# Expert matmuls of an encoder layer in pairs of weight units: the order of TensorE, ScalarE and VectorE, four raw slots and six pairs of split tiles

## What is computed

```python
xg = xt[ids]
return (jax.nn.silu(xg @ wg) * (xg @ wu)) @ wd
```

## Time and profile before

| | |
|---|---|
| time, median of 3 runs | 2544.8 us (2542.86 to 2548.42) |
| profiled execution: its own time | 2542.72 us |
| profiled execution: span | 2540.9 us |
| busy: PE | 2404.7 us, 95% |
| busy: DVE | 1933.9 us, 76% |
| busy: ACT | 1697.1 us, 67% |
| one expert, first matmul to first matmul (1329.75 to 1429.42) | 99.67 us |

### The profile page before, as it was taken

How to read it: one execution, slowest core, us unless ns; L and a number is a source line. 1 busy time by engine, 2 the same in 40 slices (tenths; PEclk the granted TensorE clock), 3 DMA queues, 4 the chain that set the end, 5 groups by cost and what they waited for, 6 DMA issues and landing times.

```text
span 2540.9 us, 51701 instructions
## 1 busy us (share of the span) xinstructions
PE 2404.7 (95%) x21830; PEld 2199.9 (87%) x21830; DVE 1933.9 (76%) x2311; ACT 1697.1 (67%) x2379; POOL 257.5 (10%) x175
## 2 busy tenths in 40 slices
PE   7999997998979949999999999999999999999997
PEld 5776884785757739999999999999999999999997
DVE  4621035884873379899999998998999999989986
ACT  6311224573443248888888888888888888888885
POOL 3312111110122000000000000000000000000000
PEclk9999996997889969999999999999999999999999
DMA  4122201002023369999999999999999999999993
GB/s 125 34 73 95 67 17 35 1 3 66 1 91 123 112 244 336 359 372 343 367 364 350 367 360 349 382 343 357 374 345 365 366 348 367 360 349 382 345 365 126
DMA packets 325114, 624.33 MB, mean 246 GB/s; under 512 B 11828, under 2 KB 48788, under 8 KB 324884
## 3 DMA queue, kind: packets, MB, share of 16 engines
q1 hardware_dynamic: 317220, 602.78, 66.6%
q0 software_dynamic: 7664, 18.25, 3.6%
HBM read 597.23 MB, written 23.69 MB: 244 GB/s over the span
## 4 chain that ended last, share of the span: by engine, by line
PE 60%; issue 3%; DVE 1%; DMA 0%; POOL 0%; POOLq 0%; ACT 0%
PE ps L1754 26%; PE ps L1782 13%; PE ps L1760 13%; PE ps L1788 6%; PE ps L1799 1%; PE ps L1736 1%; DVE wlo L1920 0%; DVE vals L1928 0%; DVE index L1931 0%; DMA out_rows<-yr,idxT 0%; DVE aff L1930 0%; POOL out_rows L1705 0%; POOL xg L1695 0%; POOLq L1674 0%; PE ps L1720 0%
## 5 line engine op out<-in xcount | busy, mean ns | idle before, releaser
L1920 DVE TENSOR_TENSOR wlo<-raw,whi 128x2048 bf16<-128x2048 f32 (+1 forms) x436 | 963.8, 2223 | 57.7 <-ACT whi L1826 54.9
L1826 ACT ACTIVATE whi<-raw 128x2048 fp32r<-128x2048 f32 (+1 forms) x436 | 804.9, 1859 | 37.6 <-PE ps L1788 37.6
L1754 PE MATMUL ps<-xx,whi 128*128 128x264 f32 x4512 | 616.2, 289 | 4.6 <-DVE xx L1971 4.6
L1754 PEld LDWEIGHTS ps<-xx,whi 128*128 128x128 f32 x4512 | 564.2, 189 | 4.8 <-DVE xx L1971 4.8
L1760 PE MATMUL ps<-xb,wlo 128*128 128x132 bf16 x4512 | 312.9, 221 | 0.0
L1782 PE MATMUL ps<-hx,whi 128*128 128x264 f32 x2256 | 312.4, 290 | 0.0
L1782 PEld LDWEIGHTS ps<-hx,whi 128*128 128x128 f32 x2256 | 283.9, 189 | 0.0
L1760 PEld LDWEIGHTS ps<-xb,wlo 128*128 128x128 bf16 x4512 | 263.2, 97 | 13.7
L1920 DVE TENSOR_TENSOR wlo_last<-raw,whi_last 128x2048 bf16<-128x2048 f32 (+1 forms) x108 | 240.6, 2228 | 13.1 <-ACT whi_last L1826 13.1
L1836 ACT ACTIVATE low<-ps 128x264 f32<-128x264 f32 x352 | 137.7, 391 | 135.8 <-PE ps L1760 122.1
L1826 ACT ACTIVATE whi_last<-raw 128x2048 fp32r<-128x2048 f32 (+1 forms) x108 | 201.5, 1866 | 9.3 <-PE ps L1788 9.3
(11 more groups left out here) (237 smaller groups left out, 3438.6 us busy)
## 6 DMA issues: line engine op xcount, KB each, us to landing
raw<-in_w_gate SPq DMA_DIRECT2D x80, 2048.0 KB, 12.6
raw<-in_w_up SPq DMA_DIRECT2D x80, 2048.0 KB, 10.3
raw<-in_w_down SPq DMA_DIRECT2D x64, 2048.0 KB, 10.9
raw<-in_w_down SPq DMA_DIRECT2D x32, 1536.0 KB, 8.2
raw<-in_w_gate SPq DMA_DIRECT2D x16, 1024.0 KB, 9.0
raw<-in_w_up SPq DMA_DIRECT2D x16, 1024.0 KB, 11.7
w<-in_w_in SPq DMA_DIRECT2D x28, 512.0 KB, 5.2
zv_rows<-qn SPq DMA_DIRECT2D x24, 256.0 KB, 2.0
```

The costliest lines, as they stand in the source:

```text
L1754: pe.matmul(banks(b + i)[:, 0:2 * C2], w[:, k, i * P:(i + 1) * P], xx[:, k], start=(k == 0), stop=False, skip_group_check=True)
L1826: nc.scalar.activation(shaped(whi[n % R_SPLIT], u), unit_raw(raw, ex, u), ACT.Copy).then_inc(hi_ready, 1)
L1920: nc.vector.tensor_tensor(shaped(wlo[n % R_SPLIT], u), unit_raw(raw, ex, u), shaped(whi[n % R_SPLIT], u).bitcast(F32), ALU.subtract).then_ ...
```

## The change

TensorE takes the units two at a time: high pass of both, then low pass of both. ScalarE and VectorE go by steps of a pair: at step p both copies or sums of pair p-1 come first, then `split_hid` of pair p-2, one split, `silu` or `gate`, and the remaining splits of the step (two in most steps, one where the table steps down at p = 4 and 8, three at p = 13 and 15). The raw ring has four slots in place of five, and the memory goes to a sixth pair of `whi` and `wlo`. `add_low` of an odd unit has one more wait, on the `gate` of the pair before (`us` must have been read), which stands ahead of it on the same engine. `split_rows` moves to the end of step 13.

```diff
-NR = 5
-R_SPLIT = 5
+NR = 4
+R_SPLIT = 6
...
-    wlo = [tiles(f"wlo{i}", [P, 2 * KD * P], BF16) for i in range(R_SPLIT - 1)]
+    wlo = [tiles(f"wlo{i}", [P, 2 * KD * P], BF16) for i in range(R_SPLIT - 2)]
...
+    wlo.append(after("wlo_next", [P, 2 * KD * P], BF16))
...
-    SPLIT_X = TURN_X + 2
+    SPLIT_X = UNITS_UP // 2 + 2
-    OUT_STEPS = {2: 0, 3: 1, 4: 2, 5: 3}
+    OUT_STEPS = {3: 0, 5: 1, 7: 2, 9: 3}
-    def lead(u):
-        return 4 if u < 6 or u >= 30 else 3 if u < 13 or u >= 27 else 2
-    def made(ex, u):
-        return min(UNITS * N_EXP, UNITS * ex + u + lead(u) + 1)
+    def made(ex, p):
+        return min(UNITS * N_EXP, UNITS * ex + 2 * p + (6 if p < 4 or p >= 15 else 5 if p < 8 or p >= 13 else 4))
```

On TensorE (`up` and `down` are each cut into a high and a low function):

```diff
-                for u in range(UNITS):
-                    if u < UNITS_UP:
-                        up(ex, u)
-                    else:
-                        down(ex, u)
+                for u in range(0, UNITS, 2):
+                    high, low = (up_high, up_low) if u < UNITS_UP else (down_high, down_low)
+                    high(ex, u)
+                    high(ex, u + 1)
+                    low(ex, u)
+                    low(ex, u + 1)
```

On ScalarE (VectorE has the same skeleton, with `add_low`, `split_low` and `gate`):

```diff
-                for u in range(UNITS):
-                    if 1 <= u <= UNITS_UP:
-                        copy_low(ex, u - 1)
+                for p in range(UNITS // 2):
+                    if 1 <= p <= PAIRS:
+                        copy_low(ex, 2 * p - 2)
+                        copy_low(ex, 2 * p - 1)
...
-                    while ahead < made(ex, u):
+                    if 2 <= p < PAIRS + 2:
+                        split_hid(ex, p - 2)
+                    if ahead < made(ex, p):
                         split_high(ahead)
                         ahead += 1
-                    if 1 <= u <= UNITS_UP and u % 2 == 1:
-                        silu(ex, u // 2)
-                    if u >= 4 and u % 2 == 0 and (u - 4) // 2 < PAIRS:
-                        split_hid(ex, (u - 4) // 2)
-                    if u == SPLIT_X and ex + 1 < N_EXP:
+                    if 1 <= p <= PAIRS:
+                        silu(ex, p - 1)
+                    while ahead < made(ex, p):
+                        split_high(ahead)
+                        ahead += 1
+                    if p == SPLIT_X and ex + 1 < N_EXP:
                         split_rows(ex + 1)
```

In VectorE's `add_low`:

```diff
+                if kind == 1 and PAIRS * ex + u // 2 >= 1:
+                    dve.wait_ge(hid_ready, PAIRS * ex + u // 2)
```

More of the change, by code:

```diff
@@ L1737, in turn_rows, with up_high @@
                 mm.then_inc(xT_done, 1)
-            def up(ex, u):
+            def up_high(ex, u):
                 t, kind = divmod(u, 2)
@@ L1755, in up, with up_low @@
                                   skip_group_check=True)
+            def up_low(ex, u):
+                n = UNITS * ex + u
                 pe.wait_ge(lo_ready, n + 1)
+                b = bank_set(ex) + 2 * (u % 2)
                 w = shaped(wlo[n % R_SPLIT], u)
@@ L1762, in up, with down_high @@
                 mm.then_inc(unit_done, 1)
-            def down(ex, u):
+            def down_high(ex, u):
                 dg, d = divmod(u - UNITS_UP, len(DOWN_PARTS))
@@ L1783, in down, with down_low @@
                                   skip_group_check=True)
+            def down_low(ex, u):
+                dg, d = divmod(u - UNITS_UP, len(DOWN_PARTS))
+                c0, cn = DOWN_PARTS[d]
+                n = UNITS * ex + u
+                b = (other_set(ex), bank_set(ex))[dg]
                 pe.wait_ge(lo_ready, n + 1)
@@ L1803, in _ @@
             for ex in range(N_EXP):
-                for u in range(UNITS):
-                    if u < UNITS_UP:
-                        up(ex, u)
-                    else:
-                        down(ex, u)
-                    if u in OUT_STEPS and ex >= 1:
-                        turn_outputs(ex - 1, OUT_STEPS[u])
-                    if u == TURN_X and ex + 1 < N_EXP:
+                for u in range(0, UNITS, 2):
[4 more added lines that the diff above has]
+                    low(ex, u + 1)
+                    if u + 1 in OUT_STEPS and ex >= 1:
+                        turn_outputs(ex - 1, OUT_STEPS[u + 1])
+                    if u + 1 == TURN_X and ex + 1 < N_EXP:
                         turn_rows(ex + 1)
@@ L1889, in _ @@
             for ex in range(N_EXP):
-                for u in range(UNITS):
-                    if 1 <= u <= UNITS_UP:
-                        copy_low(ex, u - 1)
-                    if u == DG0_END:
+                for p in range(UNITS // 2):
+                    if 1 <= p <= PAIRS:
+                        copy_low(ex, 2 * p - 2)
+                        copy_low(ex, 2 * p - 1)
+                    if 2 * p == DG0_END:
                         copy_ylow(ex, 0)
-                    if u == 0 and ex >= 1:
+                    if p == 0 and ex >= 1:
                         copy_ylow(ex - 1, 1)
-                    while ahead < made(ex, u):
+                    if 2 <= p < PAIRS + 2:
+                        split_hid(ex, p - 2)
+                    if ahead < made(ex, p):
                         split_high(ahead)
                         ahead += 1
-                    if 1 <= u <= UNITS_UP and u % 2 == 1:
-                        silu(ex, u // 2)
-                    if u >= 4 and u % 2 == 0 and (u - 4) // 2 < PAIRS:
-                        split_hid(ex, (u - 4) // 2)
-                    if u == SPLIT_X and ex + 1 < N_EXP:
+                    if 1 <= p <= PAIRS:
[4 more added lines that the diff above has]
+                    if p == SPLIT_X and ex + 1 < N_EXP:
                         split_rows(ex + 1)
-                    if u - 1 in OUT_STEPS and ex >= 1:
-                        gated_rows(ex - 1, OUT_STEPS[u - 1])
+                    if 2 * p - 1 in OUT_STEPS and ex >= 1:
+                        gated_rows(ex - 1, OUT_STEPS[2 * p - 1])
             copy_ylow(N_EXP - 1, 1)
@@ L1988, in _ @@
             for ex in range(N_EXP):
[L1989 to L1994, removed]
+                for p in range(UNITS // 2):
+                    if 1 <= p <= PAIRS:
+                        add_low(ex, 2 * p - 2)
+                        add_low(ex, 2 * p - 1)
+                    if 2 * p == DG0_END:
                         add_ylow(ex, 0)
-                    if u == 0 and ex >= 1:
+                    if p == 0 and ex >= 1:
                         add_ylow(ex - 1, 1)
-                    if u >= 5 and u % 2 == 1 and (u - 5) // 2 < PAIRS:
-                        split_hid(ex, (u - 5) // 2)
-                    while ahead < made(ex, u):
+                    if 2 <= p < PAIRS + 2:
+                        split_hid(ex, p - 2)
+                    if ahead < made(ex, p):
                         split_low(ahead)
                         ahead += 1
-                    if u == SPLIT_X and ex + 1 < N_EXP:
+                    if 1 <= p <= PAIRS:
+                        gate(ex, p - 1)
+                    while ahead < made(ex, p):
+                        split_low(ahead)
+                        ahead += 1
+                    if p == SPLIT_X and ex + 1 < N_EXP:
                         split_rows(ex + 1)
```

## The result

The changed kernel takes 2765.41 us (median of 4, 2763.85 to 2767.72) against 2544.09 us: ratio 1.0867, 95% interval 1.0849 to 1.0886. It is slower by 221 us. The forecast of 2725 us had the sign and most of the size; 40 us are missing from it.

A forecast was written before the change was run, and what follows sets the result against it. It took TensorE, busy throughout each expert, as today's bound; after the change, a chain through ScalarE's and VectorE's lists. 16 x 9.5 (up) + 15 x 2.0 (down) = 182 us on 2542.7 gave 2725 us, range 2655 to 2790.

The forecast's parts named there:

- What bounds the kernel: Expert stage, some 1,590 us: TensorE busy throughout (66.27 us up part, 33.40 down part), waiting for nothing.
- the chain: Up part, ScalarE's and VectorE's ordered lists: 14.09 us between releases, 7.05 a pair against 5.88; +9.5 us an expert.
- The pairs on TensorE: Up part: the even unit's sum comes 6.0 us after pair start, over 5.80; as a rival alone 2595 us, chance 0.06.
- The switches: TensorE, float32 to bf16 runs halved: 0.08 us saved a pair; as a rival alone 22 us gained, 2521, chance 0.04.
- The tokens: Down part: TensorE waits 2.4 us for the next expert's split tokens; down part +2.0 us, for 15 experts.
- Four slots: Raw-weight ring: taken as 0, upper end 48 us; as a rival, late loads give 2735 to 2775, chance 0.14.
- The clock: Rival: TensorE's idling drops it to 1.2 GHz, up part 128 us, total above 3400, chance 0.04; otherwise clock 1.00.
- signs of being right: Expected in the profile: PE idle some 1.2 us a pair, 2 us wait on xx, expert of 111 us, clock 1.00.
- The range: Whole kernel: own range 2658 to 2773, widened to 2655 to 2790 us.
- link error: Up part: 0.1 us more or less on each link pair, 16 x 10 x 0.1 = 16 us in all.
- the head of an expert: Start of each expert: late units there, for which the upper end was raised from 2773 to 2790 us.

## Why the prediction was right, and where it was not

- **What bounds the kernel, and the chain.** Right in place and nearly in size: 14.14 us for two pairs against 14.09, the releaser `gs`, whi ahead of DVE's first split with 1.37 us of idle time. The run with one split moved ahead shows that the chain is the cause: it takes whi out of it, two pairs fall to 12.68 us, and 165 us go. Over a whole expert's up part the links are 0.5 us longer than their sum (10.0 against 9.5).
- **The pairs on TensorE.** The forecast derived the wait from them: a sum that comes 0.2 us too late even with both engines free, and then the chain. The run with units one by one shows that they are not needed for it: the chain alone, with a whole unit between sum and reuse, costs as much. The Trainium skill asks that independent groups of matmuls rotate through the banks, so that the evacuation of one overlaps the matmuls of the next ("Perfetto Trace Analysis", section "Matmuls"); in that run they rotate as before, and the wait is there all the same, 1.87 us at the pair shown.
- **The switches.** 0.08 us a pair was taken; a pair without waits is 5.81 (5.80 forecast), and the down part alone in pairs shows 0.07.
- **The tokens.** 2.4 forecast, 2.38 measured, and shown to be `xx` by the run that takes it away. Taken away alone, it gave 6 us, as a late load took its place; with the loads shortened as well, 63.
- **Four slots.** 0 was right for the changed kernel, but the windows of 10.5 us that the forecast called slack at the end of the down part are where the loads become late (18 us at most from issue to landing) as soon as PE comes 4 us earlier.
- **The clock.** This is the term that was mis-sized. The forecast weighed it as a rival, all up parts at 1.2 GHz and above 3400 us, and put it at 0 otherwise, with a clock of 1.00 among its signs of being right. It fell in part: 34 us in all, 1.5 us a fall, once or twice an expert.
- **The range.** That 2765 lies inside 2655 to 2790 is in part luck. The forecast's own link error was 16 us; the room above that was put there for the slots and the head of an expert, which took nothing, and the clock and the longer links filled it.

## What to carry to other kernels

When two engines feed a third in order, follow the chain through their lists, from the result that is waited for back to the instruction that stands in front of it, around the loop and for every consumer: here a copy, one split and two splits of lead cost 1.2 us a pair though every engine had idle time, and one instruction moved, with a little less lead, gave back three quarters, a part of it by the clock. In this kernel grouping like passes was worth its switches (0.07 us a pair) only where no bank had to come free between the groups; there it paid a little, 0.3%, with one more split tile. Before a wait is taken out, see what stands right behind it: the tokens' wait hid late loads.

## What the runs showed of the hardware

TensorE's clock fell behind waits of some 2 us between busy stretches of 6 us, not at each of them: the pair after the same 2.4 us wait ran at 1.2 GHz for a part in 12 of 15 experts (7.3 us) and at full clock in 3 (5.8). In the run whose waits stayed at 0.9 us and less it did not fall behind the first expert's up part. A fall cost 1.5 us, and all of them 34 us in the changed kernel.
